# The scan stage of a two-block model: decayed keys on GpSimd, two products later on TensorE, a buffer for the adapter inputs

## The chip, the cores and the metric

The kernel runs on one core of one Trainium2 chip. The metric is the device time of one execution in microseconds (us), the median of several runs. Engines: TensorE (PE), VectorE (DVE), ScalarE (ACT), GpSimd (POOL) and SyncE (SP), which here only issues transfers.

## The reference

Two transformer-like blocks over 512 latent tokens with a context of 256. The first block normalises, projects, and runs two mixers (an RWKV scan and an SSM scan, each in two directions), merges them and goes through a layer of experts; the second has attention, two feed-forward parts and another scan. The change is in the RWKV part. Cut to it:

```python
def rwkv_prep(u, p):
    r, k, v, xw, xa, xg = jnp.split(u, RW_SPLITS, axis=-1)
    w_raw = p['rw_w0'] + einsum('blde,def->bldf', tanh(xw), p['rw_w2'])
    decay = exp(-exp(-softplus(-w_raw) - 0.5))
    a = sigmoid(p['rw_a0'] + einsum('blde,def->bldf', xa, p['rw_a2']))
    g = einsum('ble,ef->blf', sigmoid(xg), p['rw_g2'])
    kk = normalised(k * p['rw_kk'])                    # per head
    k_eff = k[:, :, None] * (1 + (a - 1) * p['rw_ka'])

def step(s, inp):
    sa = einsum('bhvk,bhk->bhv', s, -kk_t)
    s = s * w_t + sa * (kk_t * a_t) + v_t * k_t
    return s, einsum('bhvk,bhk->bhv', s, r_t)
```

The readout normalises the sum of both directions within each head, adds a bonus (r times k summed over a head, times v) and multiplies by the gate g.

## The kernel before

The program is a row of stages (`rwkv` is the second large one, after the first projection), each closed by a barrier of all engines. Inside a stage every engine has its own queue, written out by hand, and they meet through counted semaphores; a wait in a queue holds back all that is behind it on that engine.

`rwkv` handles the 1024 channels in 8 tiles of 128 (two heads each), one after the other, loop `for i in range(TILES)` in every queue. The 768 tokens are 6 chunks of 128, and there are two directions d. For one tile:

- SP loads the tile's rows r, k, v into `raw` (L166), then its parameters `par` and the adapter weights `lora_w` (L170, L172). Before the first tile the adapter inputs, which all tiles share, are loaded into the same `raw` (L158), and VectorE mixes neighbouring tokens from it into `small` (L224, L228).
- GpSimd weighs the centre token of each shift (`weigh_centre`, L198), VectorE adds the neighbours (`shift_step`, L241).
- `prepare`: TensorE multiplies the adapters (L503) and sums squares; ScalarE makes the decays `up` and `down` (L443, L444); VectorE makes the effective keys `keff` (L290, L293), the normalised keys `kk` (L295), `bm` (L299), then for each direction `ar` (L308, L309), the decayed keys `km` (L310), small factors, and at last the decayed `bm` (L317), which counts `ops_ready`.
- TensorE transposes (L570, two groups of values k = 0, 1 and then twelve groups, each of `ar`, `bm` and `km` of one direction and chunk), and makes the `products` of each chunk c (L584, sixteen for c below 4); VectorE multiplies them by triangular masks into `mg` (L327, for the last two chunks L331). In the same stretch VectorE interleaves the bonus (L381, L383) and the five steps of the `readout` of tile i-1 (L261, L264, L267, L270, L275).
- A triangular inverse by seven levels of doubling (`left`, `right`, `update`: L606, L623, L626, L335), which starts from identities that GpSimd copies into `work` (L205), then `solve`, `apply`, `post`, and the `hops` that carry the state from chunk to chunk, which run within the next tile's `prepare`.

For the readout of tile i-1 TensorE does, in the queue of tile i: `outputs`, `centred` (L523), `variance` (L527, waits for ScalarE's squares L413), all in `prepare`, and `bonus_gate` (L532, L533) after the products and transposes of chunk c = 1. `bonus_gate` waits for `cent_used`, which VectorE's L261 counts, since it overwrites that bank. A product of chunk c waits until the masks of chunk c-1 have read the bank.

`big` is all eight banks of PSUM; GpSimd works on SBUF tensors only. `mg` is first written by the masks of tile 0. The names `edge_*` belong to the adapter inputs.

Of the kernel before, what the change touches and what calls it, by code (L numbers as in the profile page):

```python
# [12 lines left out]
P = 128  # L13
# [36 lines left out]
def rwkv(nc, pt, loras, params, edges, consts, ya):  # L50
# [6 lines left out]
    with Stage(nc) as ctx:  # L57
# [3 lines left out]
        def sem(n):  # L61
            return ctx.sem(f"rw_{n}")
# [24 lines left out]
        fac = sb("fac", [P, 2, 6])  # L87
        ys, yq, outp = sb("ys", [P, LAT]), sb("yq", [P, LAT]), sb("outp", [P, LAT])
        big = ctx.enter_context(nc.psum_tensor("rw_big", [P, 8, BANK], F32))
        flat = big[:].rearrange("p b n -> p (b n)")  # L90
# [42 lines left out]
        norm_ready, rstd_done, run_ready, decays_done, ops_ready = (sem(n) for n in ("norm_ready", "rstd_done", "run_ready", "decays_done", "ops_ready"))  # L133
        g_ready, g_masked, tr_ready, tr_copied, eye_done = (sem(n) for n in ("g_ready", "g_masked", "tr_ready", "tr_copied", "eye_done"))
        t_ready, t_copied, xx_ready, x_updated = (sem(n) for n in ("t_ready", "t_copied", "xx_ready", "x_updated"))
        pv_ready, pv_copied, wu_ready, wu_copied, post_ready, post_done = (sem(n) for n in ("pv_ready", "pv_copied", "wu_ready", "wu_copied", "post_ready", "post_done"))
        hop_ready, hop_done, y_ready, ys_done, cent_ready, yq_done = (sem(n) for n in ("hop_ready", "hop_done", "y_ready", "ys_done", "cent_ready", "yq_done"))
        var_ready, yr_done, cent_used, bg_ready, out_done, stored = (sem(n) for n in ("var_ready", "yr_done", "cent_used", "bg_ready", "out_done", "stored"))

        def shifted_part(s, n, a, b):  # L140
            return rk[:, n, a:b] if n < 2 else val[:, s, a:b]

        with nc.Block() as block:
            @block.sync
            def _(sp):
# [4 lines left out]

                def streams(n, row, count):
                    for a, b, o in PIECES[:count]:
                        yield raw[:, n, a + 1 + o:b + 1 + o], pt[row, :, a:b]

                sp.wait_ge(cleared, 1)
                for n, (row, count) in enumerate(((XW_T, 2), (XA_T, 2), (XG_T, 1))):
                    for dst, src in streams(n, row, count):
                        sp.dma_start(dst, src).then_inc(edge_in, 16)  # L158
                for i in range(TILES):
                    if i:  # L160
                        sp.wait_ge(shifted, i)
                    else:
                        sp.wait_ge(edge_shifted, 1)
                    for n, (row, count) in enumerate(((R_T, 1), (K_T, 2), (V_T, 2))):
                        for dst, src in streams(n, row + i, count):
                            sp.dma_start(dst, src).then_inc(raw_in, 16)  # L166
                    if i >= 2:
                        sp.wait_ge(out_done, i - 1)
                        sp.dma_start(ya[i - 2], outp[:]).then_inc(stored, 16)
                    sp.dma_start(par[:, i % 2], params[i]).then_inc(par_in, 16)  # L170
                    for n, w in enumerate((w2, a2, g2)):
                        sp.dma_start(lora_w[:, i % 2, n], w[:, i * P:(i + 1) * P]).then_inc(par_in, 16)  # L172
                for i in range(TILES - 2, TILES):
# [4 lines left out]
            @block.gpsimd  # L178
            def _(pool):
                pool.memset(raw[:], 0.0)  # L180
                pool.memset(tiny[:, 0:1], -1e-12)
# [19 lines left out]
                weigh_centre(0)  # L201
                for i in range(TILES):
                    pool.wait_ge(ops_ready, 2 * i + 2)
                    for n in range(6):
                        last = pool.tensor_copy(work_ap(n * 8 * CH, [[CH, 8], [1, CH]]), ident[:].unsqueeze(1).to_broadcast([P, 8, CH]))  # L205
                    last.then_inc(eye_done, 1)
                    if i + 1 < TILES:
                        pool.wait_ge(bonus_done, i + 1)
                        weigh_centre(i + 1)

            @block.vector
            def _(dve):
                def edges_shift():
# [9 lines left out]
                    for n, a, b, o in pieces:  # L223
                        dve.tensor_scalar(small[:, n, a:b], raw[:, n, a + 1 + o:b + 1 + o], edge_col[:, n:n + 1], None, ALU.mult)  # L224
                    for m in range(2):
                        dve.drain()
                        for n, a, b, o in pieces:
                            last = dve.scalar_tensor_tensor(small[:, n, a:b], raw[:, n, a + 2 * m + o:b + 2 * m + o], edge[:, 2 * n + m:2 * n + m + 1],  # L228
                                                            small[:, n, a:b], ALU.mult, ALU.add)
# [47 lines left out]
                def prepare(i):  # L277
# [14 lines left out]
                    for d in range(2):  # L292
                        dve.tensor_tensor(keff[:, d], keff[:, d], rk[:, 1], ALU.mult)  # L293
                    dve.wait_ge(rstd_done, i + 1)
                    dve.scalar_tensor_tensor(kk[:], rk[:, 1], par[:, s, 10:11], rstd[:], ALU.mult, ALU.mult)  # L295
                    dve.drain()
                    chunks = lambda ap: ap.rearrange("p (c n) -> p c n", n=CH)
                    for d in range(2):
# [4 lines left out]
                    for d in range(2):  # L303
                        dve.wait_ge(decays_done, 2 * i + d + 1)
                        r_e = (up[:, 0, :, 1:], down[:, 1, :, 0:CH])[d]
                        a_e = (up[:, 0, :, 0:CH], down[:, 1, :, 1:])[d]
                        k_e = (down[:, 0, :, 1:], up[:, 1, :, 0:CH])[d]
                        dve.tensor_tensor(ar[:, d, :, 0], chunks(kk[:]), a_e, ALU.mult)  # L308
                        dve.tensor_tensor(ar[:, d, 0:4, 1], chunks(rk[:, 0, 0:LAT]), r_e[:, 0:4], ALU.mult)  # L309
                        dve.tensor_tensor(km[:, d], chunks(keff[:, d]), k_e, ALU.mult)  # L310
                        if d == 0:
# [3 lines left out]
                        else:  # L315
                            dve.tensor_tensor(fac[:, 1, 1:6], down[:, 1, 1:6, 0], up[:, 1, 0:5, CH], ALU.mult)
                        dve.tensor_tensor(bm[:, d], bm[:, d], k_e, ALU.mult).then_inc(ops_ready, 1)  # L317

# [50 lines left out]
                edges_shift()  # L369
                dve.wait_ge(cleared, 1)  # L370
                for k in range(10):
# [30 lines left out]
            def _(act):  # L402
# [71 lines left out]

                act.wait_ge(cleared, 1)
                act.wait_ge(const_in, 16 * 6)
# [19 lines left out]
            def _(pe):  # L496
# [38 lines left out]
                def prepare(i):  # L535
# [16 lines left out]
                    if i:  # L552
                        hop(i - 1, 4)
                        outputs(i - 1)
                        centred(i - 1)
                        variance(i - 1)

# [128 lines left out]
                for i in range(TILES):  # L686
                    prepare(i)
                    for k in range(8):
                        if k == 2:
                            pe.wait_ge(ops_ready, 2 * i + 1)  # L690
                        transposes(i, k)
                    pe.wait_ge(ops_ready, 2 * i + 2)
                    for c in range(6):
                        products(i, c)
                        transposes(i, 8 + c)
                        if i and c == 1:
                            bonus_gate(i - 1)
# [2736 lines left out]
```

## Time and profile before

| | us |
|---|---|
| median of 3 runs | 5374.77 |
| lowest, highest | 5364.8, 5377.84 |
| the profiled execution | 5348.35 |
| its span on the core | 5346.5 |
| PE, DVE, ACT, POOL busy in the span | 4436.9, 2537.0, 1577.8, 509.3 |

The span is the stretch from the first to the last instruction of one profiled execution; the scan stage is its part from about 671 to 1707 us. Matmuls are pipelined, so that TensorE's busy time is not its work at its peak.

### The profile page before, as it was taken

What the parts mean: (1) busy time and instruction counts of PE and PEld (TensorE: products, weight loads), DVE (VectorE), ACT (ScalarE), POOL (GpSimd) and SP (SyncE); (2) the same over time, 40 slices, a digit from 0 to 9 for tenths busy, and PEclk for the clock granted to TensorE, in tenths of its full rate; (3) what the DMA queues carried; (4) which work ended last, traced back from release to release, by engine and by line L of the source; (5) the groups of instructions that cost most, each with busy time, mean ns of one, the idle gap of its engine ahead of it and who ended that gap; (6) DMA issues with size and microseconds to landing.
All of it is one profiled execution on the core that took longest, in us unless ns stands there. A gap on an engine that the chain in (4) does not pass through costs nothing. (4 is left out here: it accounts for less than half of the span.)

```text
span 5346.5 us, 88289 instructions
## 1 busy us (share of the span) xinstructions
PE 4436.9 (83%) x38298; PEld 3427.1 (64%) x38298; DVE 2537.0 (47%) x3635; ACT 1577.8 (30%) x2467; POOL 509.3 (10%) x483
## 2 busy tenths in 40 slices
PE   5999968888887687865878866768999899687999
PEld 4888757777776455652222344447888788576787
DVE  4556666667664674532000033554444322476553
ACT  3222223333322453421000032433222212563322
POOL 0000011100110465000000001330000000000000
PEclk8999979999998799987999977889999999898999
DMA  6656710000001110423999531112112133212232
GB/s 227 236 197 218 265 46 14 14 14 14 14 6 36 36 50 30 173 92 120 422 422 422 232 124 52 33 52 73 64 64 69 62 110 127 76 46 84 85 102 92
DMA packets 169889, 616.55 MB, mean 115 GB/s; under 512 B 24176, under 2 KB 37489, under 8 KB 144177
## 3 DMA queue, kind: packets, MB, share of 16 engines
q1 hardware_dynamic: 156224, 551.37, 28.4%
q0 software_dynamic: 13296, 59.77, 2.8%
q8 instruction: 292, 4.78, 0.4%
q14 instruction: 77, 0.62, 0.0%
HBM read 533.32 MB, written 77.75 MB: 114 GB/s over the span
## 5 line engine op out<-in xcount | busy, mean ns | idle before, releaser
L1885 PE MATMUL f_acc<-f_a_lo,f_w_hi 128*128 128x512 f32 x4048 | 1027.3, 356 | 65.6 <-DVE f_a_lo L2107 31.6
L1885 PEld LDWEIGHTS f_acc<-f_a_lo,f_w_hi 128*128 128x128 f32 x4048 | 666.4, 190 | 189.4 <-issue 43.5
L1885 PE MATMUL f_acc<-f_a_lo,f_w_lo 128*128 128x512 f32 x2288 | 687.9, 356 | 0.0
L1874 DVE TENSOR_TENSOR f_w_lo<-f_w_raw,f_w_hi 128x1024 fp32r<-128x1024 f32 (+1 forms) x176 | 228.4, 1298 | 527.5 <-ACT f_w_hi L1869 527.5
L1885 PEld LDWEIGHTS f_acc<-f_a_lo,f_w_lo 128*128 128x128 f32 x2288 | 377.1, 189 | 62.4
L1869 ACT CAST f_w_hi<-f_w_raw 128x1024 fp32r<-128x1024 f32 (+1 forms) x176 | 194.5, 1105 | 593.5 <-DMA f_w_raw<-in_ffn_w_up 209.9
L1885 PE MATMUL i_acc<-i_x_hi,i_w_hi 128*128 128x512 f32 (+1 forms) x1024 | 306.1, 354 | 12.2 <-DVE i_x_lo L2640 11.9
L335 DVE COPY_PREDICATED rw_work<-rw_mask_x,rw_big 128x512 f32<-128x512 uint8 x288 | 238.7, 881 | 154.5 <-PE rw_big L626 149.3
L1885 PE MATMUL i_acc<-i_x_lo,i_w_hi 128*128 128x512 f32 (+1 forms) x1024 | 304.9, 353 | 0.0
L1885 PE MATMUL i_acc<-i_x_hi,i_w_lo 128*128 128x512 f32 (+1 forms) x1024 | 304.7, 353 | 0.0
L1389 PE MATMUL ex_big<-ex_w,ex_xe_now 128*64 128x512 f32 x1024 | 237.6, 619 | 76.5 <-DMA ex_w<-in_exp_w 76.5
L626 PE MATMUL rw_big<-rw_work,rw_halves 128*64 128x64 f32 x4608 | 260.7, 222 | 1.3 <-issue 1.3
L2496 DVE CUSTOM_DVE_ANT_0 i_sums<-i_mod_rows,i_mod_vec 128x1024 f32<-128x1024 f32 x192 | 236.8, 1234 | 24.9 <-issue 1.0
L623 PE MATMUL rw_big<-rw_halves,rw_work 128*64 128x64 f32 x3840 | 233.6, 222 | 1.1 <-issue 1.1
L626 PEld LDWEIGHTS rw_big<-rw_work,rw_halves 128*64 128x64 f32 x4608 | 229.3, 138 | 1.8 <-issue 1.8
L1435 DVE TENSOR_TENSOR ex_sg<-ex_sg,ex_big 128x512 f32<-128x512 f32 x16 | 11.0, 688 | 457.4 <-ACT ex_sg L1423 457.4
L1389 PEld LDWEIGHTS ex_big<-ex_w,ex_xe_now 128*64 128x64 f32 x1024 | 74.0, 142 | 238.3 <-issue 140.1
L623 PEld LDWEIGHTS rw_big<-rw_halves,rw_work 128*64 128x64 f32 x3840 | 203.8, 138 | 1.3 <-issue 1.2
L1874 DVE TENSOR_TENSOR i_w_lo<-i_w_raw,i_w_hi 128x1024 fp32r<-128x1024 f32 x84 | 102.9, 1225 | 201.5 <-ACT i_w_hi L1869 201.2
L606 PE MATMUL rw_big<-rw_work,rw_mg 128*64 128x64 f32 x5376 | 190.4, 222 | 9.0 <-DVE rw_mg L331 7.0
L1885 PEld LDWEIGHTS i_acc<-i_x_hi,i_w_hi 128*128 128x128 f32 x1024 | 168.1, 189 | 42.5 <-issue 9.3
L1885 PEld LDWEIGHTS i_acc<-i_x_lo,i_w_hi 128*128 128x128 f32 x1024 | 168.4, 189 | 26.7
(521 smaller groups left out, 8036.4 us busy)
## 6 DMA issues: line engine op xcount, KB each, us to landing
ex_w<-in_exp_w SPq DMA_DIRECT2D x192, 1024.0 KB, 17.5
i_mod_rows<-in_ada_rows SPq DMA_DIRECT2D x128, 512.0 KB, 4.9
f_w_raw<-in_ffn_w_up SPq DMA_DIRECT2D x88, 512.0 KB, 3.3
i_w_raw<-in_w_in_both SPq DMA_DIRECT2D x44, 512.0 KB, 3.7
f_w_raw<-in_ffn_w_down SPq DMA_DIRECT2D x32, 704.0 KB, 4.1
i_w_raw<-in_w_in_lat SPq DMA_DIRECT2D x40, 512.0 KB, 4.8
pt<-i_stage POOLq DMA_DIRECT2D x22, 768.0 KB, 6.3
f_w_raw<-in_hgrn_w_both SPq DMA_DIRECT2D x24, 512.0 KB, 3.2
```

Of the source, the lines that this page charges most:

```text
L335: return dve.copy_predicated(out, mask, data)
L606: last = pe.matmul(in_halves(T_BANK[n % 2], q, m, lv), mg[:, slot(BA, d, c, h), m[0]:m[1]], work_ap(xs_at + ((d * 6 + c) * 2 + h) * CH + ( ...
L623: pe.matmul(in_halves(X_BANK[n % 2], q, m, lv), work_ap(x_at + m[0], [[1, 64]]), t1_ap(n % 2, t_at + (d << lv), split(lv)), start=True, st ...
L626: last = pe.matmul(in_halves(XT_BANK[n % 2], q, m, lv), t1_ap(n % 2, t_at + m[0], [[1, 64]]), work_ap(x_at + ((1 - d) << lv), split(lv)), ...
L1389: last = pe.matmul(big[64 * half:64 * half + 64, 2 * par + m, :], xe_now[par][:, kh * KH + k], w13[kh][:, m, half, k], start=(kh == 0 and ...
L1435: dve.tensor_tensor(sg[:], sg[:], big[:, 2 * par, :], ALU.mult)
L1869: act.copy(self.view(self.w_hi, u), self.view(self.w_raw, u)).then_inc(self.hi_done, 1)
L1874: dve.tensor_tensor(self.view(self.w_lo, u), self.view(self.w_raw, u), self.view(self.w_hi, u).bitcast(F32), ALU.subtract).then_inc(self.r ...
L1885: op = pe.matmul(acc[:, a:b], part[:, k], xs[:, k0 + k, a:b], start=(first and k == 0 and part is w_hi and xs is x_hi), stop=(last and k = ...
L2496: last = dve.tensor_tensor_reduce(self.junk[:], self.slot[b % self.SLOTS][:], self.vec[:, v], 1.0, 0.0, ALU.mult, ALU.add, self.res[:, b, ...
```

## The change

Three edits in `rwkv`. First, the decayed keys `km` are made by GpSimd, as soon as `keff` and the decays are there, and no longer by VectorE; TensorE waits for them by a semaphore of their own. Second, in TensorE's queue `variance` moves behind the two value transposes, and `bonus_gate` from chunk 1 to chunk 2. Third, the adapter inputs get a buffer that lies in `mg` (`edge_raw`), which GpSimd clears first; so `raw` is free, and the first tile's rows are loaded without a wait for the mixing of the adapter inputs. Its parameters and weights are loaded ahead of them.

```diff
+        edge_raw = mg[:].rearrange("p k n -> p (k n)")[:, 0:3 * RAW].rearrange("p (n t) -> p n t", n=3)
...
+        keff_done, km_done = sem("keff_done"), sem("km_done")
...
+        chunks = lambda ap: ap.rearrange("p (c n) -> p c n", n=CH)
+
+        def key_decay(d):
+            return (down[:, 0, :, 1:], up[:, 1, :, 0:CH])[d]
...
                 sp.wait_ge(cleared, 1)
                 for n, (row, count) in enumerate(((XW_T, 2), (XA_T, 2), (XG_T, 1))):
-                    for dst, src in streams(n, row, count):
+                    for dst, src in streams(edge_raw, n, row, count):
                         sp.dma_start(dst, src).then_inc(edge_in, 16)
+                tile_weights(0)
                 for i in range(TILES):
                     if i:
                         sp.wait_ge(shifted, i)
                     else:
-                        sp.wait_ge(edge_shifted, 1)
+                        sp.wait_ge(cleared, 2)
                     for n, (row, count) in enumerate(((R_T, 1), (K_T, 2), (V_T, 2))):
-                        for dst, src in streams(n, row + i, count):
+                        for dst, src in streams(raw, n, row + i, count):
                             sp.dma_start(dst, src).then_inc(raw_in, 16)
...
-                    sp.dma_start(par[:, i % 2], params[i]).then_inc(par_in, 16)
-                    for n, w in enumerate((w2, a2, g2)):
-                        sp.dma_start(lora_w[:, i % 2, n], w[:, i * P:(i + 1) * P]).then_inc(par_in, 16)
+                    if i:
+                        tile_weights(i)
...
             def _(pool):
+                pool.memset(edge_raw, 0.0)
+                pool.drain().then_inc(cleared, 1)
                 pool.memset(raw[:], 0.0)
...
                 for i in range(TILES):
+                    pool.wait_ge(keff_done, i + 1)
+                    for d in range(2):
+                        pool.wait_ge(decays_done, 2 * i + d + 1)
+                        pool.tensor_tensor(km[:, d], chunks(keff[:, d]), key_decay(d), ALU.mult).then_inc(km_done, 1)
+                    pool.drain()
                     pool.wait_ge(ops_ready, 2 * i + 2)
...
                     for d in range(2):
-                        dve.tensor_tensor(keff[:, d], keff[:, d], rk[:, 1], ALU.mult)
+                        last = dve.tensor_tensor(keff[:, d], keff[:, d], rk[:, 1], ALU.mult)
+                    last.then_inc(keff_done, 1)
...
-                        dve.tensor_tensor(km[:, d], chunks(keff[:, d]), k_e, ALU.mult)
...
                         centred(i - 1)
-                        variance(i - 1)
...
                     for k in range(8):
                         if k == 2:
+                            if i:
+                                variance(i - 1)
                             pe.wait_ge(ops_ready, 2 * i + 1)
+                            pe.wait_ge(km_done, 2 * i + 1)
                         transposes(i, k)
                     pe.wait_ge(ops_ready, 2 * i + 2)
+                    pe.wait_ge(km_done, 2 * i + 2)
                     for c in range(6):
                         products(i, c)
                         transposes(i, 8 + c)
-                        if i and c == 1:
+                        if i and c == 2:
                             bonus_gate(i - 1)
```

`tile_weights(i)` issues the same four loads as the lines it replaces. The mixing of the adapter inputs reads `edge_raw` in place of `raw`, and the other waits for `cleared` ask for 2.

## Rows read from the trace of the kernel before

**Rows 1.** The page, its first line:

```profile
span 5346.5 us, 88289 instructions
```

**Rows 2.** Windows of core 0, the stage: busy us and instructions, clock, DMA:

```profile
core 0: us, PE busy (x) PEld busy (x) DVE busy (x) ACT busy (x) POOL busy (x), PEclk, DMA share, GB/s
671.00:1710.00 1039.00, 858.15 (x18608) 743.35 (x18608) 689.35 (x1187) 305.60 (x571) 111.83 (x116) 0.91 0.06 17
```

**Rows 3.** Timeline of DVE, tile 1: start, us, what, idle before and releaser:

```profile
837.69 1.01 DVE L295 SCALAR_TENSOR_TENSOR rw_kk<-rw_rk,rw_par,rw_rstd 128x768 f32<-128x768 f32 x1
838.79 1.83 DVE L299 SCALAR_TENSOR_TENSOR rw_bk<-rw_kk,rw_halves 128x768 f32<-128x768 f32 x2
...
842.24 0.95 DVE L310 TENSOR_TENSOR rw_bk<-rw_halves,rw_work 128x768 f32<-128x768 f32 x1
...
843.32 0.95 DVE L317 TENSOR_TENSOR rw_bk<-rw_bk,rw_work 128x768 f32<-128x768 f32 x1
...
849.69 2.48 DVE L327 TENSOR_TENSOR rw_mg<-rw_big,rw_mask_g 128x512 f32<-128x512 f32 x4 [2.13 <-PE rw_big L584]
...
853.20 2.48 DVE L327 TENSOR_TENSOR rw_mg<-rw_big,rw_mask_g 128x512 f32<-128x512 f32 x4
...
856.26 0.69 DVE L261 TENSOR_TENSOR rw_ys<-rw_big,rw_yq 128x512 f32<-128x512 f32 x1
861.74 2.48 DVE L327 TENSOR_TENSOR rw_mg<-rw_big,rw_mask_g 128x512 f32<-128x512 f32 x4 [4.79 <-PE rw_big L584]
...
864.78 2.48 DVE L327 TENSOR_TENSOR rw_mg<-rw_big,rw_mask_g 128x512 f32<-128x512 f32 x4
```

**Rows 4.** Timeline of PE, tile 1:

```profile
844.32 0.47 PE L570 MATMUL rw_big<-rw_ident,rw_ar 128*128 128x128 f32 x1 [4.44 <-DVE rw_bk L317]
...
848.50 2.00 PE L584 MATMUL rw_big<-rw_ar,rw_bk 64*128 64x256 f32 x16
...
857.00 1.15 PE L532 MATMUL rw_big<-rw_bonus,rw_blockones 128*128 128x512 f32 x2 [3.16 <-DVE rw_ys L261]
857.96 1.89 PE L533 MATMUL rw_big<-rw_small,rw_lora_w 128*128 128x512 f32 x2
```

**Rows 5.** The line of the masks, L327: its idle time in us, times:

```profile
  PE rw_big L584: 51.7, 15
```

**Rows 6.** Timeline of DVE, tile 2, the third chunk's masks:

```profile
982.28 2.49 DVE L327 TENSOR_TENSOR rw_mg<-rw_big,rw_mask_g 128x512 f32<-128x512 f32 x4 [3.15 <-PE rw_big L584]
```

**Rows 7.** Windows, behind the pause in tile 1 and in tile 2:

```profile
857.00:859.50 2.50, 2.50 (x4) 0.80 (x4) 0.00 (x0) 0.00 (x0) 0.00 (x0) 0.70 0.00 0
...
979.20:982.30 3.10, 3.10 (x16) 1.75 (x18) 0.01 (x1) 0.00 (x0) 0.00 (x0) 1.00 0.00 0
```

**Rows 8.** Timeline of PE, tile 2, the third chunk's products:

```profile
981.10 2.00 PE L584 MATMUL rw_big<-rw_ar,rw_bk 64*128 64x256 f32 x16
```

**Rows 9.** Timeline of POOL, SSM stage, VectorE idle:

```profile
1773.75 1.04 POOL L1031 TENSOR_TENSOR ss_xw<-ss_xtok,ss_kinds 128x512 f32<-128x512 f32 x1 [182.60 <-ACT ss_xtok L943]
```

**Rows 10.** The line L1046: ns min/median/max of its instructions:

```profile
L1046 POOL TENSOR_TENSOR ss_seg<-ss_seg,ss_cbt x64: 1262/1714/2786, 1799.6 to 2120.8; 128x512 f32<-128x512 f32 x64
```

**Rows 11.** Timeline of DVE, SSM stage, first without GpSimd, then beside it:

```profile
1734.79 16.16 DVE L834 SCALAR_TENSOR_TENSOR ss_xs_c<-ss_raw,ss_par,ss_xs_c 128x770 f32<-128x770 f32 x16 [0.20 <-issue]
...
1788.07 5.39 DVE L834 SCALAR_TENSOR_TENSOR ss_xs_c<-ss_raw,ss_par,ss_xs_c 128x770 f32<-128x770 f32 x4
1793.53 1.37 DVE L884 TENSOR_TENSOR ss_hf<-ss_h,ss_kinds 128x512 f32<-128x512 f32 x1
```

**Rows 12.** Timeline of all engines, the start of the scan stage:

```profile
674.00 2.33 SPq L158 DMA_DIRECT2D rw_raw<-pt  x5
...
682.54 5.81 DVE L228 SCALAR_TENSOR_TENSOR rw_small<-rw_raw,rw_edge,rw_small 128x512 f32<-128x512 f32 x10
688.38 2.22 SPq L166 DMA_DIRECT2D rw_raw<-pt  x5
...
696.01 4.01 POOL L198 TENSOR_SCALAR rw_rk<-rw_raw,rw_col 128x512 f32<-128x512 f32 x3 [0.17 <-issue]
...
702.57 1.81 DVE L241 SCALAR_TENSOR_TENSOR rw_rk<-rw_raw,rw_par,rw_rk 128x512 f32<-128x512 f32 x3 [14.22 <-POOL rw_val L198]
```

More of the change, by code:

```diff
@@ L149, in _, with streams, tile_weights @@
                     sp.dma_start(dst, src).then_inc(const_in, 16)
-                def streams(n, row, count):
+                def streams(buf, n, row, count):
                     for a, b, o in PIECES[:count]:
-                        yield raw[:, n, a + 1 + o:b + 1 + o], pt[row, :, a:b]
+                        yield buf[:, n, a + 1 + o:b + 1 + o], pt[row, :, a:b]
+                def tile_weights(i):
+                    sp.dma_start(par[:, i % 2], params[i]).then_inc(par_in, 16)
+                    for n, w in enumerate((w2, a2, g2)):
+                        sp.dma_start(lora_w[:, i % 2, n], w[:, i * P:(i + 1) * P]).then_inc(par_in, 16)
                 sp.wait_ge(cleared, 1)
                 for n, (row, count) in enumerate(((XW_T, 2), (XA_T, 2), (XG_T, 1))):
-                    for dst, src in streams(n, row, count):
+                    for dst, src in streams(edge_raw, n, row, count):
                         sp.dma_start(dst, src).then_inc(edge_in, 16)
+                tile_weights(0)
                 for i in range(TILES):
@@ L223, in edges_shift @@
                     for n, a, b, o in pieces:
-                        dve.tensor_scalar(small[:, n, a:b], raw[:, n, a + 1 + o:b + 1 + o], edge_col[:, n:n + 1], None, ALU.mult)
+                        dve.tensor_scalar(small[:, n, a:b], edge_raw[:, n, a + 1 + o:b + 1 + o], edge_col[:, n:n + 1], None, ALU.mult)
                     for m in range(2):
@@ L227, in edges_shift @@
                         for n, a, b, o in pieces:
-                            last = dve.scalar_tensor_tensor(small[:, n, a:b], raw[:, n, a + 2 * m + o:b + 2 * m + o], edge[:, 2 * n + m:2 * n + m + 1],
+                            last = dve.scalar_tensor_tensor(small[:, n, a:b], edge_raw[:, n, a + 2 * m + o:b + 2 * m + o], edge[:, 2 * n + m:2 * n + m + 1],
                                                             small[:, n, a:b], ALU.mult, ALU.add)
@@ L296, in prepare @@
                     dve.drain()
-                    chunks = lambda ap: ap.rearrange("p (c n) -> p c n", n=CH)
                     for d in range(2):
@@ L306, in prepare @@
                         a_e = (up[:, 0, :, 0:CH], down[:, 1, :, 1:])[d]
-                        k_e = (down[:, 0, :, 1:], up[:, 1, :, 0:CH])[d]
                         dve.tensor_tensor(ar[:, d, :, 0], chunks(kk[:]), a_e, ALU.mult)
                         dve.tensor_tensor(ar[:, d, 0:4, 1], chunks(rk[:, 0, 0:LAT]), r_e[:, 0:4], ALU.mult)
-                        dve.tensor_tensor(km[:, d], chunks(keff[:, d]), k_e, ALU.mult)
                         if d == 0:
@@ L316, in prepare @@
                             dve.tensor_tensor(fac[:, 1, 1:6], down[:, 1, 1:6, 0], up[:, 1, 0:5, CH], ALU.mult)
-                        dve.tensor_tensor(bm[:, d], bm[:, d], k_e, ALU.mult).then_inc(ops_ready, 1)
+                        dve.tensor_tensor(bm[:, d], bm[:, d], key_decay(d), ALU.mult).then_inc(ops_ready, 1)
                 def mask_products(i, c):
@@ L369, in _ @@
                 edges_shift()
-                dve.wait_ge(cleared, 1)
+                dve.wait_ge(cleared, 2)
                 for k in range(10):
@@ L473, in copy_t @@
                              bank_ap(T_BANK[n % 2], 0, [[256, 2], [64, 4]] + packed(lv))).then_inc(t_copied, 1)
-                act.wait_ge(cleared, 1)
+                act.wait_ge(cleared, 2)
                 act.wait_ge(const_in, 16 * 6)
```

## The prediction

> **What bounds the kernel now.** I read the page first: one core, span 5346.5 us [rows 1]. The chain that ended last, as the page gives it, lies in the last feed-forward stage, so it says nothing of the changed stage. Every stage ends in a barrier of all engines, so a microsecond saved inside one is saved in the whole, if it is saved from that stage's own chain. The windows view puts the scan stage at some 1039 us, TensorE busy for 858 of them, VectorE for 689, GpSimd for 112 [rows 2]. Eight tiles follow one another at about 122 us each.
>
> Then I read one tile in order of time, tile 1. On VectorE [rows 3] the reader is to see an unbroken run from the key product (L295) to the second L317, and TensorE standing still for 4.44 us until the first L317 lets the transposes go [rows 4]. So in this stretch VectorE is the chain. Next TensorE's products and VectorE's masks alternate. Then comes a hole: VectorE ends L261 at 856.95 and gets its next masks at 861.74, 4.79 us idle [rows 3]; TensorE was waiting 3.16 us for that same L261, because `bonus_gate` stands in its queue ahead of the third chunk's products [rows 4]. Both engines stand still in turn. The view of L327's line adds such waits up: 51.7 us in 15 waits [rows 5]. Eight of these lie before the first masks of a tile (2.13 in tile 1, 19.2 together); the other seven, one for each tile from 1 on, make 32.5 us. The least is tile 2's, 3.15 us [rows 6]. Why tile 1 has more: right behind the pause TensorE's granted clock is 0.70 of 2.4 GHz over 2.5 us, a mixture of its two levels, while in tile 2 it stays at 1.00 [rows 7]. So 4.79 - 3.15 = 1.64 us is what one such stretch at 1.2 GHz costs; most tiles are like tile 1.
>
> **`bonus_gate` one chunk later.** In tile 1, by the old times: the first half of the third products may start when half of the second masks are done, 853.20 + 1.25 = 854.45, and takes 1.0 (half of the 2.00 us of sixteen products [rows 4]); the second half runs from 855.6 to 856.6, the transposes to 857.2. VectorE goes from L261 straight into the third masks at 856.95 and is through at 859.35, and with L264 at about 859.95. `bonus_gate` finds L261 done and runs 857.2 to 859.1, taking 1.9 us as in tile 2, where it starts at 979.2 and the products follow at 981.10 [rows 7, 8]. The first half of the fourth products ends at 860.1, so the fourth masks start at about 860.2 in place of 864.78 [rows 3]: the pause of 4.79 shrinks to some 0.25. Over seven tiles: 32.5 - 7 x 0.25 = 30.7 us saved. If TensorE still falls to the low level there, 1.64 of each is given back: 19.2 us, the lower bound.
>
> **The decayed keys on GpSimd.** VectorE loses two L310 of 0.95 us at a pitch of 0.87 (the row's start to L317's, less three small ones) [rows 3]. The chain is the first L317, so 0.87 of them counts; the second L317 has slack behind the transposes. The new wait `km_done` is safe: GpSimd can begin at 837.8, when the key factors are ready, and both products are done long before 844. Nothing stands in GpSimd's queue before them; behind them are the identity copies, which wait for `ops_ready` anyway.
>
> But the two products do not run beside nothing. While GpSimd works, VectorE runs L295 and L299, which read two SBUF tensors each. The later SSM stage shows what then happens. Alone, a GpSimd product of 128x512 takes 1.04 us [rows 9], a VectorE L834 takes 16.16 / 16 = 1.01 us; with GpSimd running, four L834 take 5.39 in place of 4.04, and L884 takes 1.37 where its shape takes 0.69 elsewhere (as L261 [rows 3]) [rows 11]. That is 0.68 of delay for each GpSimd product that gets in between. For 768 columns I take 1.2 us each: 0.68 x 1.5 = 1.02 at the least, and 1.56 (1.04 x 1.5, all of it exposed) as the middle's upper end. Two make 2.4 us on the chain, against 0.87 saved: 1.5 us lost in each of eight tiles, 12.2 us. The bounds: no delay at all, because before has no such pair in this stage, gives 8 x 0.87 = 7.0 us saved; with GpSimd as slow as the quickest L1046 (1.26 x 1.5 = 1.9 [rows 10], delay about 1.6 each), 2.3 lost in each tile, 18.7 us.
>
> The Trainium skill speaks against this part: "SBUF — State Buffer", section "SBUF: two separate sides", says that a VectorE operation with two SBUF inputs and a GpSimd operation that reads SBUF exclude each other for the whole instruction. The trace agrees that they delay each other, yet the 0.68 is less than GpSimd's 1.04. By the page's rule the estimate would be 2 x 1.56 = 3.1 us in each tile, so 2.2 lost, 18 us in all in place of 12.2.
>
> **`variance` behind two transposes.** TensorE goes to the value transposes when the norms are done, some 0.4 us before the squares that `variance` needs, and the wait for L317 follows in either order: nothing, either way. If the squares' reader started later by the whole length of these transposes (1.5 us), ScalarE would still be done well before the first keys. Zero.
>
> **The first tile.** Now the adapter inputs are loaded at 674.00, VectorE mixes them until 688.35, only then do SP's five tile loads start, at 688.38, GpSimd weighs them from 696.01 to 702.46, and VectorE goes on at 702.57 [rows 12]. After: SP issues the adapter inputs to 676.3, the par and weight loads (four at 0.475, moved ahead of the tile's) to 678.2, the tile's loads to 680.4. They land 3.4 to 4.7 us after the last is issued: at about 684.2. The second clearing (another 2 us of GpSimd) ends about 675.5, in time. GpSimd then needs 6.46 us, while VectorE has 4.15 left of its mixing, which also reads two SBUF tensors. With no conflict it is done at 691 and saves 11.6. If they exclude each other, 6.46 + about 3.5 ends at 694, and 8.6 is saved. By what the SSM stage shows I take 9.
>
> **The sum.** 30.7 - 12.2 + 9 = 27.5 us. The profiled execution took 5348.35, its span 5346.5 plus 1.85 around it; it would take 5321. The shown median is 5374.77, 26 us above that single execution for nothing that the trace can tell; I apply the difference to the median: 5347.3 us.
>
> **Rivals.**
> A, the forecast, 5347 (5338 to 5360): 0.43.
> B, the keys are free: the pauses of TensorE and the small operations take GpSimd's products in. 30.7 + 7.0 + 11.6 = 49.3, 5325.5. For it: GpSimd has room of 6 us before the first keys are needed. Against: what it needs is not room but the moments between L295 and L299, and [rows 11]. 0.17.
> C, the prices are all at their upper ends: 19.2 - 18.7 + 8.6 = 9.1, 5366. For it: the new order leaves short pauses in TensorE, and L1046 shows that GpSimd's products are not all equal. Against: no pause of 3 us is left there. 0.21.
> D, the early load brings nothing, because the loads or GpSimd's weighing are held until the mixing ends: 18.5 in all, 5356. Against: neither queue has a wait left for the mixing. 0.12.
> E, slower: TensorE stays at its low level through the products of each tile, because it now stands still 1.5 us longer ahead of the transposes (4.44 to about 6). A step of sixteen products would take 4.0 in place of 2.0, a step with its transposes 4.8, where the masks set 3.05: 1.7 on each of four steps and less on the last two, some 7.5 per tile, 60 us, 5407. It decides from 27.5 / 8 = 3.4 us in a tile, two stretches of the 1.64 kind. Against: the level is already down in that pause now, and was up again when the products began. 0.07.
>
> The range 5325 to 5372 reaches to B and C. A measurement here can tell about 0.3%, 16 us. Faster by more: A nearly whole, B, most of D, little of C, 0.70. Within: 0.23. Slower: E, 0.07.
>
> **What the profile after would show.** L310 gone; two GpSimd products per tile right behind L293, each above 1.5 us; L299's pair at about 4.2 us in place of 1.83 (this is the price of the keys; at 1.83 B holds). TensorE's wait for L317 about 6 us. Before the third masks no wait, before the fourth at most 0.3, L532 without a wait, the clock at 1.00 there. VectorE's first L241 near 693.5 in place of 702.57. What would make me wrong: GpSimd's products of 3 us, `km_done` as the wait that ends last, or a lower granted clock in the products.

## The result

The changed kernel takes 5336.52 us (median of 4 runs, 5332.63 to 5342.28), the kernel before 5372.19 (4 runs): the ratio is 0.9932, 95% interval 0.9915 to 0.9948, so 28 to 46 us less. The forecast was 5347.3, 27.5 less, range 5325 to 5372. The profiled execution of the changed kernel took 5332.63, its span is 5330.8.

The two spans differ by 15.7 us only, and this number should not be read as the effect: in the profiled execution of the changed kernel the scan stage begins at 679.70, before it began at 671.26, though nothing ahead of it was changed, and what follows the stage took 5.1 us more. The stage by itself is the fair comparison. From GpSimd's first clearing to the first clearing of the next stage (VectorE's) it takes 1007.13 us (before, between the same two instructions, 671.26 to 1707.67, 1036.41), which is 29.3 less. The windows view of the changed kernel:

```profile
core 0: us, PE busy (x) PEld busy (x) DVE busy (x) ACT busy (x) POOL busy (x), PEclk, DMA share, GB/s
679.70:1686.83 1007.13, 840.66 (x18608) 734.74 (x18608) 695.34 (x1171) 305.76 (x571) 150.11 (x133) 0.92 0.06 17
```

Between the same two instructions VectorE was busy for 687.03 us before ([rows 2] has 689.35 for a slightly longer stretch). Now the 16 products are gone from it, and it is *longer* busy, 695.34. Part by part, in the order of the stage. The start of the stage after (all engines, start and duration):

```profile
679.70 2.02 POOL L192 MEMSET rw_mg<- 128x2313 f32 x1 [7.10 <-POOLq L30]
...
690.95 6.73 DVE L247 SCALAR_TENSOR_TENSOR rw_small<-rw_mg,rw_edge,rw_small 128x512 f32<-128x512 f32 x10
692.57 5.03 POOL L212 TENSOR_SCALAR rw_rk<-rw_raw,rw_col 128x512 f32<-128x512 f32 x3 [1.65 <-DMA rw_raw<-pt]
...
700.14 1.81 DVE L260 SCALAR_TENSOR_TENSOR rw_rk<-rw_raw,rw_par,rw_rk 128x512 f32<-128x512 f32 x3 [2.46 <-POOL rw_val L212]
```

VectorE goes on with the first tile 20.44 us after the clearing, before 702.57 - 671.26 = 31.31 [rows 12]. The early load is worth 10.9 us. The rows also show its price: GpSimd's three operations take 5.03 us where they took 4.01, and VectorE's mixing beside them 6.73 where it took 5.81 [rows 12].

Tile 1 on VectorE after, where L315, L318, L326, L334, L344, L280 are what L295, L299, L308, L317, L327, L261 were:

```profile
836.83 1.01 DVE L315 SCALAR_TENSOR_TENSOR rw_kk<-rw_rk,rw_par,rw_rstd 128x768 f32<-128x768 f32 x1
837.93 4.57 DVE L318 SCALAR_TENSOR_TENSOR rw_bk<-rw_kk,rw_halves 128x768 f32<-128x768 f32 x2
842.64 0.96 DVE L326 TENSOR_TENSOR rw_ar<-rw_kk,rw_work 128x768 f32<-128x768 f32 x1
...
844.33 0.95 DVE L334 TENSOR_TENSOR rw_bk<-rw_bk,rw_work 128x768 f32<-128x768 f32 x1
...
850.70 2.48 DVE L344 TENSOR_TENSOR rw_mg<-rw_big,rw_mask_g 128x512 f32<-128x512 f32 x4 [3.00 <-PE rw_big L600]
...
857.40 0.69 DVE L280 TENSOR_TENSOR rw_ys<-rw_big,rw_yq 128x512 f32<-128x512 f32 x1
858.00 2.48 DVE L344 TENSOR_TENSOR rw_mg<-rw_big,rw_mask_g 128x512 f32<-128x512 f32 x4
860.57 0.55 DVE L283 TENSOR_SCALAR rw_ys<-rw_ys,rw_par 128x512 f32<-128x512 f32 x1
861.32 2.48 DVE L344 TENSOR_TENSOR rw_mg<-rw_big,rw_mask_g 128x512 f32<-128x512 f32 x4 [0.20 <-PE rw_big L600]
```

The pair of L299 takes 4.57 us in place of 1.83 [rows 3]: that is the move of the keys, 2.74 us of stall for 0.87 saved. GpSimd's side of it, on its timeline:

```profile
837.00 4.68 POOL L220 TENSOR_TENSOR rw_bk<-rw_halves,rw_work 128x768 f32<-128x768 f32 x2 [90.02 <-DVE rw_halves L312]
```

The same two pairs instruction by instruction, from narrower windows of the two timelines:

```profile
837.00 2.33 POOL L220 TENSOR_TENSOR rw_bk<-rw_halves,rw_work 128x768 f32<-128x768 f32 x1 [90.02 <-DVE rw_halves L312]
837.93 2.22 DVE L318 SCALAR_TENSOR_TENSOR rw_bk<-rw_kk,rw_halves 128x768 f32<-128x768 f32 x1
839.30 2.39 POOL L220 TENSOR_TENSOR rw_bk<-rw_halves,rw_work 128x768 f32<-128x768 f32 x1
840.07 2.43 DVE L318 SCALAR_TENSOR_TENSOR rw_bk<-rw_kk,rw_halves 128x768 f32<-128x768 f32 x1
```

They can be read as the two engines taking turns. VectorE's L315 ends at 837.84 and GpSimd's first product 1.49 later (839.33); then L318 ends 0.82 later (840.15), the second product 1.54 later (841.69), the second L318 0.81 later (842.50). GpSimd's durations of 2.33 and 2.39 would then hold its own waiting; 1.49 and 1.54 are close to the 1.56 estimated for a product that runs alone (1.04 x 1.5, [rows 9]).

The third chunk's masks follow L280 with no idle time, the fourth's wait 0.20; from the first masks to the fourth it is 10.62 us, before 15.09 [rows 3]. TensorE's timeline in the same tile:

```profile
833.72 0.88 PE L586 MATMUL rw_big<-rw_ident,rw_val 128*128 128x128 f32 x6 [1.60 <-ACT rw_rstd L457]
835.67 2.08 PE L544 MATMUL rw_big<-rw_yq,rw_blockones 128*128 128x512 f32 x2 [1.08 <-ACT rw_yq L430]
845.34 0.48 PE L586 MATMUL rw_big<-rw_ident,rw_ar 128*128 128x128 f32 x1 [7.59 <-DVE rw_bk L334]
...
855.68 2.33 PE L600 MATMUL rw_big<-rw_ar,rw_bk 64*128 64x256 f32 x16 [0.83 <-DVE rw_mg L344]
...
858.33 1.02 PE L549 MATMUL rw_big<-rw_bonus,rw_blockones 128*128 128x512 f32 x2
859.19 1.02 PE L550 MATMUL rw_big<-rw_small,rw_lora_w 128*128 128x512 f32 x2
860.14 2.00 PE L600 MATMUL rw_big<-rw_ar,rw_bk 64*128 64x256 f32 x16
```

`bonus_gate` no longer waits. And the windows view of the same place, to be read against tile 1's 0.70 in [rows 7], shows TensorE at its upper level:

```profile
858.30:860.80 2.50, 2.50 (x12) 1.22 (x12) 2.40 (x5) 0.54 (x2) 0.00 (x0) 1.00 0.00 0
```

To add up all tiles, three distances were read on VectorE's timeline of each tile: from the scan operation that opens `prepare` to the first L317 ("keys"), from the first masks to the first update of the inverse, L335 ("masks"), and the stage as a whole. The same is done for each kernel below. The fourth distance, from the scan to the first update, takes in both and the way between them, and is added up over all eight tiles.

| kernel | stage | to the first scan | keys, tiles 1 to 7 | masks, tiles 1 to 7 | sum of masks, tiles 1 to 7 | scan to update, 8 tiles |
|---|---|---|---|---|---|---|
| before | 1036.41 | 39.00 | 13.97 | 21.07 to 24.07 | 159.1 | 342.2 |
| changed | 1007.13 | 28.13 | 15.85 | 17.92 to 18.42 | 127.1 | 326.6 |

So: 10.9 from the start, 159.1 - 127.1 = 32.0 from `bonus_gate`, and 8 x 1.88 = 15.0 lost by the keys. 10.9 + 32.0 - 15.0 = 27.9 of the stage's 29.3. The rest is made of small parts of both signs: the way from L317 to the first masks is 1.5 longer over the eight tiles, and the last tile's end, behind its last update, takes 41.0 in place of 43.4, though nothing was changed in it.

The way from L317 to the first masks (6.37 to 7.59 us before, 6.37 to 7.61 in the changed kernel) goes with the clock that TensorE was granted in it. Before, in tile 1 and in tile 4, which has the longest:

```profile
843.32:849.69 6.37, 5.37 (x29) 3.99 (x30) 4.24 (x9) 3.19 (x12) 2.07 (x3) 0.65 0.00 0
1212.45:1220.04 7.59, 6.58 (x28) 4.88 (x30) 4.24 (x8) 3.24 (x12) 3.29 (x4) 0.52 0.01 2
```

### The profile page after: what moved, and what is told of

Same layout as the page of the kernel before. It is cut to its first block and busy times, and to the rows that moved or that the text cites. A ratio compares the mean times of both kernels' runs of the same rounds, so it can differ in the third digit from the quotient of the medians.

```text
span 5330.8 us, 88307 instructions
## 1 busy us (share of the span) xinstructions
PE 4427.5 (83%) x38298; PEld 3420.2 (64%) x38298; DVE 2545.1 (48%) x3619; ACT 1579.1 (30%) x2467; POOL 547.5 (10%) x500
## 5 line engine op out<-in xcount | busy, mean ns | idle before, releaser
L1905 PEld LDWEIGHTS i_acc<-i_x_lo,i_w_hi 128*128 128x128 f32 x1024 | 167.9, 189 | 27.9
```

Of the source, the lines that this page charges most:

```text
L1905: op = pe.matmul(acc[:, a:b], part[:, k], xs[:, k0 + k, a:b], start=(first and k == 0 and part is w_hi and xs is x_hi), stop=(last and k = ...
```

## The experiments

The theory after this reading: `bonus_gate` and the early load give 43 us and the keys take 15 of them back, since GpSimd's products hold up VectorE's operations with two tensors in SBUF. The rival: VectorE's shorter work shortens its chain, and the stalls are taken up elsewhere. And within the theory: what of GpSimd's work is it that VectorE waits for, its length, its reading, or that it is there at all?

### One part alone, or all but one

**bonus_only**, on the kernel before:

```diff
-                        if i and c == 1:
+                        if i and c == 2:
                             bonus_gate(i - 1)
```

Expected:

> The kernel before with bonus_gate after chunk 2 and nothing else. The theory (the pause of 3 us on TensorE and the stretch of low clock behind it both go): about 31 us less than before in all, L327 idle 51.7 us going down to about 21, L532 without a wait, in tile 1 the fourth chunk's masks 10.6 us after the first's (before 15.1). Rival (only the wait goes, the low clock stays for a stretch in each tile): about 20 us less.

Measured: 5341.34 us (6 runs) against 5370.29 (20 runs), ratio 0.9948 (0.9931 to 0.9965), 19 to 37 us less. The idle time before the masks, in us and times, with the eight waits before a tile's first masks still in it:

```profile
  PE rw_big L584: 23.9, 15
```

and `bonus_gate` in tile 1, without a wait and at 1.02 us a pair:

```profile
871.60 1.02 PE L532 MATMUL rw_big<-rw_bonus,rw_blockones 128*128 128x512 f32 x2
872.47 1.02 PE L533 MATMUL rw_big<-rw_small,rw_lora_w 128*128 128x512 f32 x2
```

The masks' distances add up to 129.5, 29.6 less than before, near the theory's 31. Before, the granted clock behind the pause was low in six of the seven tiles; here it is 1.00 in all seven. The stage as a whole is only 22.2 shorter (1014.19). The other 7 us lie in parts that the edit does not touch: 3.2 on the way from the first L317 to the masks, 3.7 in the inverse (from its first update to VectorE's first instruction behind it, 57.5 to 59.5 us in a tile before, 58.1 to 60.6 here) and 0.5 in the last tile's end. All three vary from kernel to kernel where nothing was changed in them, and with one profile of each it is not shown whether the later `bonus_gate` has a part in it. The 23.9 us, too, are more than the 21 that were expected, by the waits before the first masks.

**keys_only**, on the kernel before, the semaphores `keff_done` and `km_done` added, for which TensorE waits as in the change:

```diff
+                    pool.wait_ge(keff_done, i + 1)
+                    for d in range(2):
+                        pool.wait_ge(decays_done, 2 * i + d + 1)
+                        pool.tensor_tensor(km[:, d], chunks(keff[:, d]), key_decay(d), ALU.mult).then_inc(km_done, 1)
+                    pool.drain()
...
-                        dve.tensor_tensor(km[:, d], chunks(keff[:, d]), k_e, ALU.mult)
```

Expected:

> The kernel before with only the decayed keys moved to GpSimd. The theory (each of GpSimd's two products holds VectorE's two-input operations up for its reading): L299's pair 4.6 us in place of 1.83, the first L317 1.9 us later in each of eight tiles, 15 us slower than before. Rival (VectorE works less, so the chain is 0.87 us shorter in each tile, and the stalls seen are taken up elsewhere): 7 us faster.

Measured: 5385.39 (9 runs) against 5370.29, ratio 1.0031 (1.0019 to 1.0043): 10 to 23 us *slower*. The stage takes 1052.19, 15.8 more, and the scan-to-L317 distance is 15.84 or 15.85 in every tile from 1 on, as in the changed kernel. From the scan to the update it is 357.3 over the eight tiles, 15.1 more. VectorE's pair in tile 1:

```profile
850.25 4.58 DVE L311 SCALAR_TENSOR_TENSOR rw_bk<-rw_kk,rw_halves 128x768 f32<-128x768 f32 x2
```

This part of the change does harm by itself, by what the theory said, and the rival falls.

**load_only**, the early load alone (`edge_raw`, the second clearing, `tile_weights(0)` ahead):

```diff
+                tile_weights(0)
...
-                        sp.wait_ge(edge_shifted, 1)
+                        sp.wait_ge(cleared, 2)
```

Expected:

> Only the own buffer of the adapter inputs and the early load of the first tile; keys, variance and bonus_gate as before. The theory: first L241 about 20.5 us after the stage's first instruction on GpSimd in place of 31.3, 11 us less in all. Rival (something later in the first tile waits all the same, for instance for the adapter products): 5 us or less.

Measured: 5362.84 (12 runs) against 5370.29, ratio 0.9987 (0.9974 to 0.9999), 1 to 14 us less; the executions scatter too much for more. Its profile decides: VectorE's first L241 (here L255, at 703.98) comes 20.50 us after the clearing at 683.48, and the stage takes 1023.72, 12.7 less. With the start's 10.8 the theory holds.

```profile
703.98 1.81 DVE L255 SCALAR_TENSOR_TENSOR rw_rk<-rw_raw,rw_par,rw_rk 128x512 f32<-128x512 f32 x3 [2.46 <-POOL rw_val L212]
```

**no_keys**, the changed kernel with the product back on VectorE:

```diff
+                        dve.tensor_tensor(km[:, d], chunks(keff[:, d]), key_decay(d), ALU.mult)
...
-                        pool.tensor_tensor(km[:, d], chunks(keff[:, d]), key_decay(d), ALU.mult).then_inc(km_done, 1)
```

Expected:

> The changed kernel with the decayed keys back on VectorE: early load, variance and bonus_gate as changed. If the keys' move costs 15 us, this is 15 us faster than the changed kernel: about 42 to 50 us below before (ratio 0.991 to 0.992). If the move gains, it is 5 to 7 us slower than the changed kernel, about 25 to 30 below before.

Measured: 5331.63 (6 runs), ratio 0.9937 (0.9920 to 0.9954). This is 25 to 43 us below before, where 42 to 50 was expected, and by the medians alone it cannot be told from the changed kernel. In its profile the keys' distance is back at 13.97 (13.96 to 13.97, tiles 1 to 7), the stage takes 998.88, 8.3 less than the changed kernel's 1007.13 and 11.2 less than its second profile below. Of the 15 us, then, 8 to 11 are seen in the stage; the inverse took 473 us over the eight tiles here and 467 in the changed kernel, which is the scatter named above. From the scan to the first update, where the keys' move acts, it is 312.3 against 326.6, so 14.3 of the 15 are there.

**after_again**, the changed kernel once more, beside the next:

> The changed kernel once more, beside the kernels of this group. Ratio to before 0.992 to 0.995; the stage from GpSimd's first clearing to the next stage's clearing about 1007 us, give or take 5, against 1036 before.

Measured: 5336.42 (6 runs) against 5368.69 (11 runs), ratio 0.9946 (0.9929 to 0.9963); stage 1010.09. Together with the first result the effect is 20 to 46 us by the medians and 26 to 29 by the stage.

**variance_back**, the changed kernel with `variance` in front of the value transposes:

```diff
                         centred(i - 1)
+                        variance(i - 1)
...
-                            if i:
-                                variance(i - 1)
```

> The changed kernel with variance back in front of the value transposes. The theory (no one waits for either): from the scan to the first L317 15.85 us and from there to the masks 6.4 to 7.6, as in the changed kernel; nothing gained or lost. Rival (variance was part of what shortened the stage): the distances grow by up to 1.5 us in each tile.

Measured, one execution: the distances are 15.84 or 15.85 and 6.4 to 7.6, the stage 1010.11. Nothing waits for it in either place; TensorE only stands still in another place, as the timeline shows (6.31 ahead of the transposes in place of 7.59, 3.55 ahead of `variance` in place of 1.60 and 1.08 around the value transposes):

```profile
834.01 2.08 PE L544 MATMUL rw_big<-rw_yq,rw_blockones 128*128 128x512 f32 x2 [3.55 <-ACT rw_yq L430]
843.68 0.48 PE L587 MATMUL rw_big<-rw_ident,rw_ar 128*128 128x128 f32 x1 [6.31 <-DVE rw_bk L334]
```

**bonus_late**, the changed kernel with `if i and c == 3` before `bonus_gate`:

> The changed kernel with bonus_gate still one chunk later, after chunk 3. VectorE needs its result right behind the fourth masks (L267), so the wait comes back on VectorE: about 1.9 us of bonus_gate in each tile, less what the earlier fourth masks give (0.2), masks to update 19.5 to 20 us in place of 18.2. Rival (it only matters that it is late enough): 18.2 or less.

Measured, one execution: 18.16 to 18.64 in place of 17.92 to 18.42, a wait of 0.39 us on VectorE, stage 1014.14. The expectation, 19.5 to 20, was wrong by about 1.3 us in each tile. It forgot the fourth masks, 2.5 us of VectorE's work between the products and L286, beside which `bonus_gate` runs.

```profile
860.90 0.69 DVE L286 TENSOR_TENSOR rw_yq<-rw_big,rw_val 128x512 f32<-128x512 f32 x1 [0.39 <-PE rw_big L550]
```

So the place is not sharp: one chunk later cures the pause, two chunks later nearly as well.

### What VectorE waits for

**keys_memset**, the changed kernel with a constant in place of the product, which leaves the decayed keys out:

```diff
-                        pool.tensor_tensor(km[:, d], chunks(keff[:, d]), key_decay(d), ALU.mult).then_inc(km_done, 1)
+                        pool.memset(km[:, d], 0.01).then_inc(km_done, 1)
```

> The changed kernel with GpSimd writing a constant into the decayed keys in place of the product, at the same place in its queue; the product is left out. If what delays VectorE is GpSimd reading the tensors (exclusion on a reading port): L299's pair back at 1.83 and from the scan to the first L317 13.1 us (15.85 in the changed kernel, 13.97 before). If any work of GpSimd on the same memory delays VectorE, the pair stays above 2.5.

Measured, GpSimd and then VectorE in tile 1:

```profile
836.68 1.42 POOL L220 MEMSET rw_bk<- 128x768 f32 x2 [90.49 <-DVE rw_halves L312]
```

```profile
836.54 1.01 DVE L315 SCALAR_TENSOR_TENSOR rw_kk<-rw_rk,rw_par,rw_rstd 128x768 f32<-128x768 f32 x1
837.63 1.83 DVE L318 SCALAR_TENSOR_TENSOR rw_bk<-rw_kk,rw_halves 128x768 f32<-128x768 f32 x2
```

GpSimd writes while VectorE runs an operation with two inputs, and VectorE's durations are those of [rows 3] to the last digit. The keys' distance is 13.10: 13.97 less the 0.87 of L310. This writing does no harm.

**keys_scaled**, the same with one tensor read, which leaves the decay out:

```diff
-                        pool.tensor_tensor(km[:, d], chunks(keff[:, d]), key_decay(d), ALU.mult).then_inc(km_done, 1)
+                        pool.tensor_scalar(km[:, d], chunks(keff[:, d]), 0.01, None, ALU.mult).then_inc(km_done, 1)
```

> The changed kernel with GpSimd multiplying the effective keys by a constant (one tensor read in place of two); the decay is left out. L198 takes 1.57 us for 512 columns of such an operation, so it should take some 2.3 us for 768, longer than the product of two tensors alone (1.5 by the SSM stage). If exclusion holds for the length of the instruction, the pair of L299 goes up to about 1.83 + 2 x 2.2 = 6.2 us; if the price goes by what is read, half of the changed kernel's: about 3.2.

Measured:

```profile
839.92 5.19 POOL L220 TENSOR_SCALAR rw_bk<-rw_halves 128x768 f32<-128x768 f32 x2 [91.13 <-DVE rw_halves L312]
```

```profile
839.75 1.01 DVE L315 SCALAR_TENSOR_TENSOR rw_kk<-rw_rk,rw_par,rw_rstd 128x768 f32<-128x768 f32 x1
840.85 2.28 DVE L318 SCALAR_TENSOR_TENSOR rw_bk<-rw_kk,rw_halves 128x768 f32<-128x768 f32 x2
843.27 1.35 DVE L326 TENSOR_TENSOR rw_ar<-rw_kk,rw_work 128x768 f32<-128x768 f32 x1
```

Here GpSimd's two operations are longer than the products (5.19 us in place of 4.68), and the delay is 0.45 on L318 and 0.39 on L326, 0.84 in all, in place of 2.74; the keys' distance is 13.95. The first expectation (exclusion for the length of the instruction, a pair of 6.2 us) is refuted, and the second, half the price, was too high as well: it is a third. The windows that part the pairs show it most plainly:

```profile
839.92 2.83 POOL L220 TENSOR_SCALAR rw_bk<-rw_halves 128x768 f32<-128x768 f32 x1 [91.13 <-DVE rw_halves L312]
840.85 1.41 DVE L318 SCALAR_TENSOR_TENSOR rw_bk<-rw_kk,rw_halves 128x768 f32<-128x768 f32 x1
842.18 0.95 DVE L318 SCALAR_TENSOR_TENSOR rw_bk<-rw_kk,rw_halves 128x768 f32<-128x768 f32 x1
842.73 2.39 POOL L220 TENSOR_SCALAR rw_bk<-rw_halves 128x768 f32<-128x768 f32 x1
```

GpSimd's first scaling lasts from 839.92 to 842.75 and holds up only the first L318; the second one takes 0.95 us, as it does alone, though it runs beside it. Each of GpSimd's instructions of 768 columns costs VectorE this much: the constant 0, the scaling 0.42, the product 1.37 us. So the price does not go by how long GpSimd's record lasts. It rises with the number of tensors that GpSimd reads, but the operation was another one each time, and the decays lie with gaps in memory where the keys do not; which of these makes the product so dear, no run here parts. For the product the rows fit turns of full length (1.49 and 1.54 against 0.82, above), for the scaling they do not.

### VectorE's operands in another order

**first_direction_first**, the changed kernel without the keys' move, and VectorE's operands in another order:

```diff
-                    for d in range(2):
-                        dve.scalar_tensor_tensor(bm[:, d], chunks(kk[:]), -1.0, chunks(aa[:, d]), ALU.mult, ALU.mult)
-                    dve.drain()
...
                     for d in range(2):
...
+                        dve.scalar_tensor_tensor(bm[:, d], chunks(kk[:]), -1.0, chunks(aa[:, d]), ALU.mult, ALU.mult)
+                        dve.wait_ge(decays_done, 2 * i + d + 1)
                         dve.tensor_tensor(ar[:, d, :, 0], chunks(kk[:]), a_e, ALU.mult)
+                        dve.tensor_tensor(km[:, d], chunks(keff[:, d]), key_decay(d), ALU.mult)
                         if d == 0:
+                            dve.drain()
+                            dve.tensor_tensor(bm[:, d], bm[:, d], key_decay(d), ALU.mult).then_inc(ops_ready, 1)
+                            dve.tensor_tensor(ar[:, d, 0:4, 1], chunks(rk[:, 0, 0:LAT]), r_e[:, 0:4], ALU.mult)
...
```

> Early load, variance and bonus_gate as changed, keys on VectorE, and on VectorE the first direction's operands finished before the second's are begun, the r product and the small factors behind the first counting of ops_ready. If VectorE's chain up to that first counting sets TensorE's start: one L299 (0.87), the r product (0.60) and three small ones (0.22) come off it, 1.5 us earlier than with the keys on VectorE alone (12.4 in place of 13.97 us from the scan to it); the second direction then takes some 5 us behind it against 4.6 of transposes, so about 1 us of each tile is kept: 7 to 9 us less than the variant with the keys on VectorE, the shortest stage of all, about 991. Rival: the second direction's operands become what the products wait for, and nothing is left.

Measured: 5326.46 (6 runs) against 5368.69, ratio 0.9923 (0.9901 to 0.9945), 30 to 53 us less than before. The stage:

```profile
683.12:1675.05 991.93, 848.70 (x18608) 738.88 (x18608) 690.14 (x1186) 305.63 (x571) 115.27 (x117) 0.93 0.06 17
```

991.93, where 991 was expected: 44.5 less than before, 15 to 18 less than the two profiles of the changed kernel, and 7.0 less than no_keys. The scan-to-L317 distance is 12.2 (13.97), but 1.0 of each 1.76 comes back, most of it on the way to the masks, where the products wait for the second direction, and the first tile is 0.9 us longer. From the scan to the update it is 308.1 over the eight tiles against 312.3 in no_keys: the new order is worth 4.3 us, not 7 to 9. That the stage came out at 991 is in part luck, since the inverse was 5 us shorter here than in no_keys. By the medians it is 10 us faster than the changed kernel of the same group, which their intervals do not separate; by the stage it is the shortest of those that compute the whole, and from scan to update 18.5 us shorter than the changed kernel.

The stage in each kernel, from the profiles:

| kernel | stage, us | keys, tiles 1 to 7 | sum of masks, tiles 1 to 7 | scan to update, 8 tiles |
|---|---|---|---|---|
| keys_only | 1052.19 | 15.85 | 159.0 | 357.3 |
| load_only | 1023.72 | 13.97 | 159.0 | 343.2 |
| bonus_only | 1014.19 | 13.97 | 129.5 | 315.6 |
| after_again | 1010.09 | 15.85 | 126.8 | 326.6 |
| no_keys | 998.88 | 13.97 | 127.8 | 312.3 |
| keys_scaled (decay left out) | 997.27 | 13.95 | 125.8 | 314.3 |
| keys_memset (keys left out) | 993.92 | 13.10 | 126.3 | 303.7 |
| first_direction_first | 991.93 | 12.2 | 129.4 | 308.1 |

## Why the prediction was right

The direction, the sum (27.5, measured 29.3 in the stage and 35.7 by the medians) and the three mechanisms hold. By its steps:

- **`bonus_gate`.** 30.7 was forecast, 32.0 is seen, with the fourth masks at 10.6 us behind the first, as worked out. The stretch of low clock did not come back, so the lower bound of 19.2 played no part. bonus_only shows it alone.
- **The keys.** The mechanism is right, the term was too small: 2.4 us of delay, 2.74 measured, 1.5 lost in each tile, 1.88 measured, 12.2 in all against 15.0. The term was scaled from products of 512 columns by 1.5; 1.37 each lies in its range of 1.02 to 1.56. As for the reason, the forecast only had that the two delay each other. The runs with a constant and with one input show that the price is not set by the length of GpSimd's record, and that a constant, for which GpSimd reads nothing, is free.
- **The Trainium skill.** Its page "SBUF — State Buffer", section "SBUF: two separate sides", was right that the two engines are in each other's way, and right to speak of a GpSimd operation that reads: the constant delayed nothing. The whole-instruction exclusion does not hold for the scaling: two operations of GpSimd, 5.19 us together, cost VectorE 0.84. For the product itself it fits better than the prediction allowed: taken one by one, the instructions end as if the engines took turns of 1.49 and 1.54 us. Its estimate for this case, 3.1 us per tile, was above the measured 2.74, the forecast's 2.4 below it by as much.
- **The first tile.** 9 was taken, 10.9 measured. The slowing of both sides is there, 1.02 and 0.92 us, but it is nearer to no conflict (11.6) than to full exclusion (8.6), which fits keys_scaled, since GpSimd's operation there reads one tensor only.
- **`variance`.** Zero, as variance_back shows. TensorE's pause ahead of the transposes was forecast at some 6 us and is 7.59; that took in the later L317, but not that the value transposes now run inside an earlier wait (with `variance` back in its place it is 6.31). It changed nothing else.
- **The rivals.** B falls by keys_only, the keys have a price. C's prices did not occur. D falls by load_only. E falls by the windows: the products of tile 1 are at the upper level again in the changed kernel, behind a pause of 7.59 us. Through its first four steps of products the granted clock is 1.00:

```profile
849.52:864.00 14.48, 12.95 (x91) 8.23 (x92) 12.92 (x21) 2.81 (x11) 4.21 (x5) 1.00 0.00 1
```

The sum was right partly by two small errors of opposite sign, the keys by -2.8 and the start and `bonus_gate` by +3.2. The 35.7 by the medians holds 6 us more than the stage shows; they are not accounted for, and 29.3 lies within the interval of the ratio too.

## What to carry to other kernels

An edit of several parts should be read part by part even when the whole is faster: here one part costs 15 of the 43 us that the others bring, and the faster kernel is the one without it. Moving work from a full engine to an empty one only pays if the empty one can run beside it; before moving an operation with two SBUF inputs to GpSimd, look which of VectorE's operations run at that time. Where the scatter of the whole hides an effect, add up the distances in which the edit acts: of the 15 us expected of the keys the stage shows 8 to 11 and the scan-to-update distance 14.3, while the medians cannot tell. An instruction that waits in a queue ahead of work that others need (`bonus_gate`) costs its wait, and then once more by the low clock behind the pause: one place later cured both.

## What the runs showed of the hardware

- A GpSimd instruction of 768 columns, float32, beside VectorE operations with two SBUF inputs cost VectorE 1.37 us when it was a product of two tensors, 0.42 when it was a scaling of one, though that instruction is recorded as longer, and nothing when it wrote a constant. That a slow GpSimd instruction can be the cheaper neighbour was not expected.
- By the granted clock in the traces a pause of 3 us on TensorE was followed by a stretch at 1.2 GHz in six of seven tiles before, and in five of seven in keys_only and in load_only; with the pause gone this stretch was gone in all seven tiles, in each of the kernels that moved `bonus_gate`.
- The way from the first L317 to the first masks took 6.37 us at a granted clock of 0.65 and 7.59 at 0.52.
- The inverse's 57 to 61 us per tile vary at an unchanged code, between tiles of one execution and from kernel to kernel, at a granted clock of 1.00 throughout. Over eight tiles this makes 6 to 7 us, and it is part of what hides an effect of 8 us in the medians. Its cause was not tried.
